# Attention of the first block on one core: query halves exchanged by transfers inside the on-chip memory, and softmax steps in other slots

## What is computed

```python
def rope(x, positions):
    ...
    x1, x2 = xf[..., :half], xf[..., half:]
    return jnp.concatenate([x1 * cos - x2 * sin, x2 * cos + x1 * sin], axis=-1).astype(x.dtype)

def swa_with_sinks(q, k, v, sinks):
    ...
    scores = jnp.where(valid[None, :, None, None], scores, -jnp.inf)
    sink = sinks.astype(jnp.float32).reshape(SWA_KV_HEADS, SWA_GROUP)[None, None, :, :, None, None]
    m = jnp.maximum(jnp.max(scores, axis=-1, keepdims=True), sink)
    p = jnp.exp(scores - m)
    probs = p / (jnp.sum(p, axis=-1, keepdims=True) + jnp.exp(sink - m))
    o = jnp.einsum("bnhgqk,bnkhd->bnqhgd", probs.astype(v.dtype), vals,
                   preferred_element_type=jnp.float32)
```

## Time and profile before

| what | value |
|---|---|
| device time, median of 3 runs | 3942.58 us (3937.88 to 3949.83) |
| profiled execution, first to last instruction | 3936.2 us |
| PE busy | 3791.8 us, 96% |
| DVE, ACT busy | 2786.2 us, 71%; 1888.4 us, 48% |
| one attention step g (g = 2, 3) | 59.16 us |

### The profile page before, as it was taken

The page is one execution under the profiler, slowest core; times in us unless marked ns, Lnnn a source line. Parts: engine busy times, 40 slices in busy tenths (PEclk is TensorE's granted clock), DMA queues, the critical chain, the costliest instruction groups (busy, mean ns, idle before and its releaser), DMA issues.

```text
span 3936.2 us, 73085 instructions
## 1 busy us (share of the span) xinstructions
PE 3791.8 (96%) x28822; PEld 3598.6 (91%) x28822; DVE 2786.2 (71%) x3780; ACT 1888.4 (48%) x2849; POOL 185.9 (5%) x188
## 2 busy tenths in 40 slices
PE   1999999999999999999999999999999999999998
PEld 1999999999999999999999999999988798989888
DVE  7788887757777778888675675565576666666676
ACT  1546455335544355555533554454565433334365
POOL 0111211000000012121000000000000000000000
PEclk8999999999999999999999999999999999999999
DMA  9533433863368843434385434445534445555543
GB/s 396 182 141 138 143 135 141 304 220 142 140 236 311 297 148 139 144 138 147 139 317 198 140 140 169 182 162 179 187 111 168 171 171 193 182 183 183 182 149 129
DMA packets 137169, 716.41 MB, mean 182 GB/s; under 512 B 37184, under 2 KB 37632, under 8 KB 60800
## 3 DMA queue, kind: packets, MB, share of 16 engines
q1 hardware_dynamic: 111456, 631.31, 44.6%
q10 hardware_dynamic: 25504, 82.13, 5.9%
HBM read 711.22 MB, written 2.16 MB: 181 GB/s over the span
## 4 chain that ended last, share of the span: by engine, by line
PE 84%; DVE 7%; ACT 4%; issue 3%; DMA 2%; DVEq 0%; ACTq 0%; SPq 0%
PE bank L278 17%; PE bank L280 17%; PE bank L279 17%; PE bank L295 8%; PE bank L296 4%; PE bank L2346 2%; PE bank L2348 2%; PE bank L317 2%; PE bank L2347 2%; ACT Wh L343 2%; PE bank L321 2%; DMA raw<-in_ada 1%; DVE Wl L349 1%; PE bank L319 1%; PE bank L320 1%
## 5 line engine op out<-in xcount | busy, mean ns | idle before, releaser
L343 ACT CAST Wh<-raw 128x1024 fp32r<-128x1024 f32 x1124 | 1169.1, 1047 | 1664.1 <-PE bank L280 1226.0
L349 DVE TENSOR_TENSOR Wl<-raw,Wh 128x1024 fp32r<-128x1024 f32 x1124 | 1383.0, 1235 | 788.9 <-ACT Wh L343 784.1
L278 PE MATMUL bank<-H,Wh 128*128 128x256 f32 x5440 | 1597.0, 294 | 2.0 <-DVE Wl L349 1.2
L279 PE MATMUL bank<-H,Wh 128*128 128x256 f32 x5440 | 1538.4, 283 | 0.0
L280 PE MATMUL bank<-H,Wl 128*128 128x256 f32 x5440 | 1538.0, 283 | 0.0
L278 PEld LDWEIGHTS bank<-H,Wh 128*128 128x128 f32 x5440 | 1041.9, 192 | 29.2 <-issue 17.5
L279 PEld LDWEIGHTS bank<-H,Wh 128*128 128x128 f32 x5440 | 1042.5, 192 | 11.3 <-issue 8.6
L280 PEld LDWEIGHTS bank<-H,Wl 128*128 128x128 f32 x5440 | 1041.5, 191 | 0.0
L295 PE MATMUL bank<-H,Wh 128*128 128x512 f32 x1280 | 449.9, 396 | 6.4 <-DVE WS L336 6.1
L296 PE MATMUL bank<-H,Wl 128*128 128x256 f32 x1280 | 358.6, 280 | 0.0
L295 PEld LDWEIGHTS bank<-H,Wh 128*128 128x128 f32 x1280 | 240.6, 188 | 66.2 <-issue 5.5
(11 more groups left out here) (413 smaller groups left out, 4776.7 us busy)
## 6 DMA issues: line engine op xcount, KB each, us to landing
raw<-in_stream SPq DMA_DIRECT2D x560, 1024.0 KB, 4.8
WS<-in_ada ACTq DMA_DIRECT2D x94, 512.0 KB, 6.1
raw<-in_ada SPq DMA_DIRECT2D x32, 1024.0 KB, 7.6
gm_more<-in_ada ACTq DMA_DIRECT2D x20, 512.0 KB, 6.9
WS<-rows_d ACTq DMA_DIRECT2D x16, 512.0 KB, 5.2
KR<-in_ada ACTq DMA_DIRECT2D x14, 512.0 KB, 6.9
raw<-in_stream SPq DMA_DIRECT2D x8, 512.0 KB, 6.8
X<-in_x_t SPq DMA_DIRECT2D x1, 2048.0 KB, 17.0
```

Source lines behind the costliest of these rows:

```text
L278: pe.matmul(out[:, 0:T], wh, xh[:, kt, :], start=first, stop=False)
L279: pe.matmul(out[:, 0:T], wh, xl[:, kt, :], start=False, stop=False)
L343: act.copy(Wh[:, n % 4, :], raw[:, (sbk + 2) % 4, k * (D // 2):(k + 1) * (D // 2)]).then_inc(hi_ready, 1)
L349: dve.tensor_tensor(Wl[:, n % 4, :], raw[:, (sbk + 2) % 4, k * (D // 2):(k + 1) * (D // 2)], Wh[:, n % 4, :].bitcast(F32), ALU.subtract).t ...
```

## The change

It does four things in this stage, and nothing elsewhere except dropping the second call of `tail` in `pe_end`:

1. The two `swap` matmuls go. After blocks 5 and 7 have been copied to `qx`, ACT issues four transfers each (`swap(x)`) from `qx` to a new buffer `qs`, 32 partitions by 512 elements each. DVE rotates in two halves, `rotated(0)` at slot 15 and `rotated(1)` in slot 3 of the next step.
2. The exponentials stand in slot 4t+1, ahead of the cast. The probabilities stand in slot 4t+2, the transposes ahead of slot 4t+3, the value matmuls ahead of slot 4t+4, and the output steps in slots 4t+4 and 4t+5.
3. The copies to `PT` become `turned(n)`: in slot 4t+3, behind the cast of that slot.
4. The value matmuls are written head by head in alternation.

```diff
+                if n % 4 == 3:
+                    t = n // 4
                     S.wait(pe, "dve", f"prob{t}", r)
                     ...transposes...
+                if n % 4 == 0 and n:
+                    t = n // 4 - 1
+                    S.wait(pe, "act", f"PT{t}", r)
+                    halves = [slice(64 * h, 64 * h + 64) for h in range(2)]
+                    for h in range(2):
+                        pe.matmul(B[4][halves[h], 0:P], vg[:, 0, :], PT[:, h, 0:P], start=True, stop=True)
+                    for h in range(2):
+                        pe.matmul(B[4][halves[h], P:2 * P], vg[:, 0, :], PT[:, h, P:2 * P], start=True, stop=False)
+                    for h in range(2):
+                        m = pe.matmul(B[4][halves[h], P:2 * P], vg[:, 1, :], PT[:, h, 2 * P:3 * P], start=False, stop=True)
...
-            st_rot.start("pe")
-            pe.wait_ge(tile_taken, l * TILES + 100 + g * 8 + 8 + 2)
-            for i in range(2):
-                m = pe.matmul(B[i][:, :], const("swap"), qx[:, 2 * i:2 * i + 2, :], start=True, stop=True)
-            st_rot.done(m, "pe", "swap")
...
+            def swap(x):
+                act.wait_ge(tile_taken, f0 + (4 + 2 * x + 1 + 3))
+                for quarter in range(4):
+                    to, of_ = 32 * quarter, 32 * (quarter ^ 1)
+                    act.dma_start(qs[to:to + 32, 2 * x:2 * x + 2, :], qx[of_:of_ + 32, 2 * x:2 * x + 2, :]).then_inc(turned_in[x], 16)
...
                 if n < 15:
                     act_cast(act, q + b // 4, b % 4, k)
+                if chain:
+                    turned(n)
...
+            def rotated(x, turn):
+                R, two = st_rot, slice(2 * x, 2 * x + 2)
+                dve.wait_ge(turned_in[x], 64 * turn + 64)
+                R.done(dve.tensor_tensor(qr[:, two, :], qx[:, two, :], ROPE[:, 0:1, :].to_broadcast([P, 2, T]), ALU.mult), "dve", f"cos{x}")
+                R.done(dve.tensor_tensor(qs[:, two, :], qs[:, two, :], ROPE[:, 1:2, :].to_broadcast([P, 2, T]), ALU.mult), "dve", f"sin{x}")
+                R.wait(dve, "dve", f"sin{x}", turn)
+                R.done(dve.tensor_tensor(qr[:, two, :], qr[:, two, :], qs[:, two, :], ALU.add), "dve", f"turned{x}")
```

More of the change, by code:

```diff
@@ L222, in build_program @@
         st_swa, st_rot = stage("swa"), stage("swa_turn")
+        turned_in = [sem(f"turned_queries{x}_in") for x in range(2)]
         st_na, st_rgset, st_rg = stage("na"), stage("rgset"), stage("rg", seeded=("pe", "dve"))
@@ L1418, in ready @@
                     st_gdn.wait(pe, "dve", "o_lo", l * PAIRS + PAIRS - 1)
-                if half and kt in (4, 10):
-                    tail(16 if kt == 4 else 17)
+                if half and kt == 4:
+                    tail(16)
                 if half and kt >= KT - 4:
@@ L1568, in pe_swa @@
                 before(16)
-            st_rot.start("pe")
-            pe.wait_ge(tile_taken, l * TILES + 100 + g * 8 + 8 + 2)
-            for i in range(2):
-                m = pe.matmul(B[i][:, :], const("swap"), qx[:, 2 * i:2 * i + 2, :], start=True, stop=True)
-            st_rot.done(m, "pe", "swap")
-            if chain:
-                before(17)
         def act_swa(act, l, g, chain):
-            S, q = st_swa, l * Q_LAYER + Q_PRE + Q_GDN + Q_END + 2 * g
+            S, q, f0 = st_swa, l * Q_LAYER + Q_PRE + Q_GDN + Q_END + 2 * g, l * TILES + 100 + g * 8
+            last = isinstance(g, int) and g == KV
             if chain:
@@ L1615, in act_swa @@
                         S.wait(act, "dve", "rot", r)
+                    if chain and b == (2 if last else 6):
+                        st_rot.wait(act, "dve", "turned1", r)
                     act_tile(act, q + b // 4, b % 4)
                     if b == 0:
-                        act.wait_ge(tile_taken, l * TILES + 100 + g * 8 + 2)
-                    if isinstance(g, int) and g == KV:
+                        act.wait_ge(tile_taken, f0 + 2)
+                    if last:
                         act.activation(gates8[:, b, :], G[b % 2][:, 0:T], ACT.Tanh, scale=0.5).then_inc(tile_taken, 1)
[L1621 to L1625, removed]
+                    else:
+                        dst = zx[:, b, :] if b < 4 else qx[:, b - 4, :]
+                        act.copy(dst, G[b % 2][:, 0:T]).then_inc(tile_taken, 1)
+                        if b == 5:
+                            swap(0)
+                        if b == 7:
+                            swap(1)
                     if n == 15:
                         act_cast(act, q + 1, 3, 1)
[L1628 to L1632, removed]
+            if not last:
                 st_rot.start("act")
+                if chain:
+                    S.wait(act, "pe", "pv3", r)
                 st_rot.done(act.copy(kg, KR[:, bass.ds(g, 1), :].rearrange("p a b -> p (a b)")), "act", "kg")
             if chain:
-                work(18)
+                work(17)
         def dve_swa(dve, l, g, chain):
             S, q = st_swa, l * Q_LAYER + Q_PRE + Q_GDN + Q_END + 2 * g
+            last = isinstance(g, int) and g == KV
             if chain:
@@ L1679, in before, with after @@
                         S.done(x, "dve", f"prob{t}" if m == 3 else f"p{t}_{m}")
-                if n % 4 == 2 and n > 2:
-                    t -= 1
+            def after(n):
+                t = n // 4 - 1
+                if n % 4 == 0 and n:
                     S.wait(dve, "pe", f"pv{t}", r)
@@ L1686, in before @@
                     S.done(dve.tensor_tensor(of, B[4][:, 0:T], zsb[:, t, :], ALU.mult), "dve", f"o{t}")
-            def after(n):
-                if n % 4 == 2 and n > 2:
-                    t = n // 4 - 1
+                if n % 4 == 1 and n > 1:
                     S.wait(dve, "act", f"hi{t}", r)
@@ L1703, in dve_swa @@
                     after(n)
+                if chain and n == 3:
+                    rotated(1, r)
+                if not last and n == 15:
+                    st_rot.start("dve")
+                    dve.wait_ge(tile_taken, l * TILES + 100 + g * 8 + 8)
+                    rotated(0, l * KV + g)
             if chain:
                 dve_low(dve, q + 1, 3, 1)
[L1706 to L1719, removed]
+                after(16)
+                after(17)
         fin_sq, fin_acc = ws(1024, 4, 2, T), ws(3072, 2, T)
```

22 lines of the change are left out of this document (13 added, 9 removed).

## The result

The changed kernel takes 4040.8 us (median of 4 runs, 4036.3 to 4042.3) beside 3940.2 us for the kernel before: a ratio of 1.0247, 95% interval 1.0230 to 1.0265. It is slower, as forecast, but by 100 us and not by 67: the time lies 9 us above the upper end of the range. The profiled span went from 3936.2 to 4040.5 us, by 104.3.

What follows compares the result with a forecast made beforehand. PE, busy 96% of the span, was taken as the bound; savings of 11.3 and 8.6 us against losses of 49.4, 21.1 and 16.8 us gave +67.4 us, so 4010 us from 3942.6, range 3996 to 4032.

Steps and rivals of the forecast that it cites:

- part 1: PE's swap of 1.88 us leaves six chain steps (g = 1, 2, 3 in two layers): 11.3 us saved.
- part 2: Value matmuls in alternation on PE: 0.27 us saved in each of 32 groups, 8.6 us saved, bounds 0 to 11.8.
- part 3: PE's value matmuls wait for ACT's PT copies behind the cast: 2.06 us idle, 24 times, 49.4 us lost.
- parts 4 and 5: Transposes wait for probabilities, 0.66 us for 32 head pairs (21.1 us); late step ends add 2.8 us six times (16.8 us).
- part 5: Step end: ACT's four transfer issues delay the next step's first pair, 16.8 us lost; nothing counted for step g = 1.
- The walk from scores to probabilities: Chain from scores' end to PE's transposes: 6.49 us needed against 5.83 us in two slots, so a 0.66 us wait.
- The clock falls: Rival: PE's granted clock halves behind the six long waits, 1.7 us lost each, 10 us, giving 4020 us; chance 0.17.
- a case of 51 us: Rival: the shorter 2.06 us PE waits also drop the clock, 30 x 1.7 = 51 us, giving 4061 us; chance 0.03.
- the rival for the long waits: Clock at half behind six PE waits of 3.5 us at the transposes: 10 us lost, 4020 us; chance 0.17.
- The price of a transfer's issue: Each of four transfers issued by ACT at a step's end holds it 0.40 us (0.355 to 0.443), 1.6 us together.

## Why the prediction was wrong

The direction and the mechanism were right; the size was not. Point by point, with the sums of the profiled span:

| step | forecast us | measured us |
|---|---|---|
| part 1, swap gone from six steps | -11.3 | -11.3 (no such instruction left) |
| part 2, alternation | -8.6 | 32 x 0.27 = -8.6 |
| part 3, wait for the copies | +49.4 | 18 x 2.05 + 6 x 2.11 = +49.6 |
| parts 4 and 5, waits at the transposes | +37.9 | 24 x 0.61 + 6 x 3.74 = +37.1 |
| part 5, key copy late | 0 | 6 x 0.67 = +4.0 |
| part 5, entry into step 1 | 0 | 2 x 1.0 = +2.0 |
| clock | 0 | +29 (half of 58 us, an estimate) |
| sum | +67.4 | +102 |

The two attention stages are 99.4 us longer. Without the clock the terms make 72.8, so the stages leave 27 us for it, close to the estimate of 29.

**Parts 1 to 4 held.** The reading that mattered, that a copy behind a cast comes after the very matmuls that should hide it, gave the wait within 0.01 us. The walk from scores to probabilities was 0.03 us off. (The first pair of step 1 has no wait in either layer: its slots ran partly at half clock, behind the long wait at the entry, so the chain had more time. That makes 30 waits, not 32.) The 3.75 us of the first pairs beside 3.5 are partly luck: the transfers held ACT 0.9 us longer than forecast, but PE itself was held some 0.7 us at the key copy and so asked later.

**The clock is the step that failed.** The sum put it at nothing. "The clock falls" was a rival with a chance of 0.17, priced at 10 us, and only for the six long waits. For the 24 of 2.06 us I wrote that one row, a wait of 2.35 us behind which the clock stayed, speaks against it, and gave 0.03 to a case of 51 us. One row was taken for a rule. In the changed kernel the clock fell at all six long waits (for 6.8 us at two of them), at the two entries into step 1, and behind 8 of the 24 short waits. By half of the time at half clock this is 13.7, 3.4 and 13.7 us, less 1.7 that the kernel before lost as well: 29 us. So the rival for the long waits came true, and the short waits, which I had all but ruled out, cost as much again. The kernel with the 2.05 us waits alone shows that they are enough: the clock fell behind 12 of 24. The row of the kernel before could not give this share; but the question was open and the loop asks it 30 times, so the range should have taken in a good part of the 51 us.

The Trainium skill ("TensorE: Matmul & The Clock Gate", HAM oscillation) warns that gaps which return with each tile throttle the engine again and again. Its example has longer gaps than these of 2 us; here the short ones throttled it too, but not each time.

**The price of a transfer's issue** was a smaller miss. I took 0.40 us from the nearest row; the new ones take 0.61, outside the 0.355 to 0.443 that I took for bounds. All instructions of this line in the changed kernel (ns min/median/max), and their time to landing:

```profile
L1613 ACTq DMA_DIRECT2D gm_more<-WS x64: 514/612/1542, 875.5 to 2427.5; - x64
...
DMA to landing us min/median/max: 1.9/2.1/6.5
```

With 2.5 us in place of 1.6, the first pairs wait 0.25 us more, PE waits for the key copy, and the entry into step 1 is late: 1.5, 4.0 and 2.0 us, some 7 in all. I had followed the chain to DVE's mask and forgotten that the key copy, in the same queue, is wanted by the scores. With issues of 0.40 us it would have been done at +3.5 us of the forecast's own count, 0.2 ahead of the scores at +3.7, so this zero hung on that price.

## What to carry to other kernels

Before a result is wanted one slot earlier, walk back from it through its engine's queue: if a cast or any other instruction ahead of it waits for the matmuls that were meant as cover, there is no cover, and the wait is the sum of what stands behind them. Swapping two statements, or asking for the result in the middle of the cover instead of at its end, removed such waits here. A repeated idle gap on PE costs more than its length: 24 gaps of 2.05 us alone cost 49 us by their length and some 15 more through the clock, and matmuls with unused results in the gaps gave part of such a loss back. Whether the clock falls behind a given gap could not be told from one row.

## What the runs showed of the hardware that I had not expected

- In the kernel with equal waits of 2.05 us (1.9 us idle) 16 to 18 us apart, three in each group, the granted clock fell to half behind 12 of 24 waits, for 3.4 us each, 41 us in all; the same kernel without these waits had no fall in the chain steps. In the changed kernel, with three filler matmuls in each such wait and five in the long ones, the clock fell behind none of them, though up to 1.5 us of each stayed idle.
- Issuing a transfer of 32 partitions by 2 KB inside the on-chip memory held ACT's queue for 0.61 us at the median, longer than the 0.33 us of the 1 MB weight blocks on SP's queue in the kernel before or the 0.42 us of the earlier trace rows. It landed after 2.1 us.
- Breaks of a slot by small matmuls cost PE little: 14.20 us for a head pair with two breaks, beside 14.01 without.
